# A memory-attention and top-4-of-32 expert step on one core: shorter path from the attention to the first expert, first refills of the weight ring in halves, a reordered last turn

## What is computed (reference, cut)

```python
x = x + mixer(rmsnorm(x, g_mix), ...)
x = x + cross_attn(rmsnorm(x, g_xattn), mk, mv, w_q, w_xo)   # 4 heads of 256
h = rmsnorm(x, g_moe)
logits = h @ w_router + b_router
top_logit, top_e = lax.top_k(logits, 4)
gates = softmax(top_logit)
# for each expert e and its tokens:
gu = xb @ w1[e] + b1[e]; gate, up = split(gu); gate = min(gate, 7); up = clip(up, -7, 7)
y = ((up + 1) * gate * sigmoid(1.702 * gate)) @ w2[e] + b2[e]
x = x + sum(gate weight * y over a token's experts)
return rmsnorm(x, g_final), ...
```

## Time and profile before

| | |
|---|---|
| median of 3 runs | 1202.78 us (1202.31 to 1203.34) |
| the profiled execution, its own time | 1203.28 us |
| its span in the profile | 1201.3 us |
| PE busy | 1162.1 us (97%) |
| weight loads of PE (beside matmuls) | 608.4 us (51%) |
| DVE / ACT / POOL busy | 306.8 / 155.2 / 28.0 us |
| bytes moved by DMA | 458.34 MB, mean 382 GB/s |
| PE's granted clock, mean over the span | 0.998 of full |

### The profile page before, as it was taken

How to read it: one execution, slowest core, us unless ns; L and a number is a source line. 1 busy time by engine, 2 the same in 40 slices (tenths; PEclk the granted TensorE clock), 3 DMA queues, 4 the chain that set the end, 5 groups by cost and what they waited for, 6 DMA issues and landing times.

```text
span 1201.3 us, 14815 instructions
## 1 busy us (share of the span) xinstructions
PE 1162.1 (97%) x5935; PEld 608.4 (51%) x5935; DVE 306.8 (26%) x636; ACT 155.2 (13%) x240; POOL 28.0 (2%) x62
## 2 busy tenths in 40 slices
PE   9999999999999999999999999999999999999986
PEld 8888887684434344444444343434343434343433
DVE  5114532342221212122122212121212121212124
ACT  2011011031101111011011111101110111101012
POOL 0000000000000000000000000000000000000000
PEclk9999999999999999999999999999999999999999
DMA  9963343998999999999999999999999999999994
GB/s 368 400 228 141 117 157 139 427 392 296 423 421 429 427 428 429 428 428 428 428 428 428 429 428 428 429 428 428 429 428 428 428 428 428 429 428 428 427 427 188
DMA packets 39102, 458.34 MB, mean 382 GB/s; under 512 B 5888, under 2 KB 6656, under 8 KB 8096
## 3 DMA queue, kind: packets, MB, share of 16 engines
q1 hardware_dynamic: 36144, 454.12, 90.2%
q10 hardware_dynamic: 2928, 3.80, 0.9%
HBM read 454.41 MB, written 3.23 MB: 381 GB/s over the span
## 4 chain that ended last, share of the span: by engine, by line
PE 51%; DMA 26%; DVE 1%; issue 0%; ACT 0%; SPq 0%; DVEq 0%; ACTq 0%
PE ps L1262 27%; DMA ring<-in_w_gu 26%; PE ps L1357 11%; PE ps L1228 6%; PE ps L1253 4%; PE ps L1272 2%; PE ps L1369 0%; PE ps L1306 0%; DVE resid L1001 0%; DVE arena L987 0%; PE ps L1375 0%; ACT arena L618 0%; DVE arena L929 0%; PE ps L1015 0%; DVE arena L899 0%
## 5 line engine op out<-in xcount | busy, mean ns | idle before, releaser
L1262 PE MATMUL ps<-ring,arena 128*64 128x512 f32 x1536 | 350.4, 598 | 15.5 <-DMA ring<-in_w_gu 11.7
L1262 PEld LDWEIGHTS ps<-ring,arena 128*64 128x64 f32 x1536 | 104.0, 136 | 211.0 <-issue 193.8
L1051 PE MATMUL ps<-arena,ring 128*128 128x264 f32 (+1 forms) x800 | 179.2, 386 | 1.4 <-issue 1.0
L1357 PE MATMUL ps<-ring,arena 128*64 128x512 f32 x768 | 171.1, 594 | 4.0 <-DMA ring<-in_w_dn 3.0
L1051 PEld LDWEIGHTS ps<-arena,ring 128*128 128x128 f32 x800 | 151.6, 190 | 27.2 <-issue 1.6
L1262 PE MATMUL ps<-arena 128*64 128x512 f32 x512 | 116.7, 598 | 4.6 <-DMA arena<-in_w_gu 4.4
L987 DVE COPY arena<-ps 64x512 f32<-64x512 f32 x32 | 22.2, 694 | 365.4 <-PE ps L1357 365.4
L1357 PEld LDWEIGHTS ps<-ring,arena 128*64 128x64 f32 x768 | 54.1, 137 | 112.4 <-issue 99.6
L1228 PEld LDWEIGHTS ps<-arena 128*128 128x128 f32 x768 | 93.2, 197 | 13.8 <-issue 13.8
L938 DVE TENSOR_TENSOR resid<-resid,ps 128x264 f32<-128x264 f32 x128 | 53.2, 429 | 181.4 <-PE ps L1253 180.9
L1228 PE MATMUL ps<-arena 128*128 128x128 f32 x768 | 97.6, 284 | 0.0
(11 more groups left out here) (190 smaller groups left out, 490.9 us busy)
## 6 DMA issues: line engine op xcount, KB each, us to landing
ring<-in_w_gu SPq DMA_DIRECT2D x96, 2048.0 KB, 32.2
ring<-in_w_dn SPq DMA_DIRECT2D x47, 2048.0 KB, 32.7
arena<-in_w_gu SPq DMA_DIRECT2D x32, 2048.0 KB, 32.4
arena<-in_w_dn SPq DMA_DIRECT2D x15, 2048.0 KB, 32.7
ring<-in_w_in SPq DMA_DIRECT2D x10, 1024.0 KB, 27.4
ring<-in_kc SPq DMA_DIRECT2D x8, 1024.0 KB, 4.8
ring<-in_vc SPq DMA_DIRECT2D x8, 1024.0 KB, 5.1
ring<-in_w_v SPq DMA_DIRECT2D x4, 1024.0 KB, 22.6
```

The costliest lines, as they stand in the source:

```text
L1051: last = mm(b[:, 0:width], w[:, k, P * (m % 2):P * (m % 2) + P], source(k), start=(k == 0), stop=(k == KT - 1))
L1262: last = mm(ps[64 * h:64 * h + 64, n, :], tile[:, k, SLOTS * half:SLOTS * half + SLOTS], w[:, at:at + 512], start=(k == 0), stop=(k == KT ...
L1357: last = mm(ps[64 * h:64 * h + 64, 4, :], hid[i % 2][:, k, :], w[:, at:at + 512], start=(k == 0), stop=(k == KT - 1))
```

## The change

**Attention.** Scores go by pairs of heads instead of by token tiles, and the second pair alone waits for the last queries. The first "out" projection waits for the gated convolution piece by piece instead of as a whole. Normalising all four score tiles comes ahead of the samples' maximum. "oS" moves ahead of "o" 6 and 7, which then stand after "oS" and after "oST"; the first "xo" waits for its inputs piece by piece.

**Router.** `g_moe` is multiplied into the router weights early (on DVE, once the parameters are in), so "lg" reads the residual itself, and its last part is cut in four. ACT instead of DVE copies "lg". A square is added as soon as it is there. The table load for the square root is moved ahead of "xo", and the early load for the exponential is dropped. The four chosen logits are now marked by a copy, three `match_replace` and one comparison. The count of tokens per expert becomes a group of matmuls of its own ("free0"). Four PE fillers (`keep_busy`) are dropped. ACT writes `h_tok` in the layout in which the gather reads it.

**First expert.** It writes banks 6 and 7 instead of 0 and 1. The transposition of the gates and the two gathers of the upper half move in between the halves of its second and third units. DVE copies the first gathered quarter ahead of the gates.

**Ring.** The first units are loaded in the order 0, 2, 3, 4, 5, 1, 6, 7. The first eight refills, numbers 8 to 15, all go in two halves of 1 MB, the first half as soon as the first half of the unit before was used.

**Loop.** In even experts the gather stands between the two down units instead of ahead of them.

**Last turn.** Combinations stand one place earlier, so none is left between the last gate/up unit and its transposition. The last down goes to bank 5 and arrives in five pieces (two, two, two, one and one tiles of 128 rows); its result is copied in halves of 256 columns.

```diff
-          + [("o", m) for m in range(4)] + ["pST"] + [("o", m) for m in range(4, 8)] + ["oS", "oST"] + [("xo", m) for m in range(8)]
-          + ["lg", "ssq2", "lgT"] + [("htok", n) for n in range(6)] + ["rank", ...
+          + [("o", m) for m in range(4)] + ["pST", ("o", 4), ("o", 5), "oS", ("o", 6), "oST", ("o", 7)]
+          + [("xo", m) for m in range(8)]
+          + ["lg", ("htok", 0), "ssq2", "lgT"] + [("htok", n) for n in range(1, 6)] + ["rank", ...
...
+LAST_PARTS = [(0, 2), (2, 4), (4, 6), (6, 7), (7, 8)]
...
+            for n in (0, 2, 3, 4, 5, 1, 6, 7):
+                first_units(n)
...
             for n in range(RING_UNITS):
-                first_units(n)
-            sp.wait_ge(half_used, 1)
...
+                for part in range(2):
+                    if part == 0:
+                        sp.wait_ge(half_used, n + 1)
+                    elif n % 4 == 3:
+                        sp.wait_ge(gu_done, n // 4 + 1)
+                    else:
+                        sp.wait_ge(w_used, n - n // 4 + 1)
+                    half = slice(SLOT * part, SLOT * part + SLOT)
+                    sp.dma_start(unit_buffer(n)[:, half], rows_of(RING_UNITS + n)[:, half]).then_inc(
+                        unit_landed[n] if part else half_landed[n], 16)
...
-            TTN(eq[:], lg[:], fourth, ALU.is_equal).then_inc(dve_step, 1)
-            link(nc.vector.tensor_reduce(cnt3, gt[:], AX.X, ALU.add))
+            link(copy(top4[:, :, 0:TOPK], top8[:, :, 0:TOPK]))
             for t in range(TT):
-                ins = nc.vector.tensor_tensor_scan(cum[:, t, :], ones[:, 0:NE], eq[:, t, :], cnt3[:, t:t + 1],
-                                                   ALU.mult, ALU.add)
+                nc.vector.match_replace(struck[:, t, :], top4[:, t, :], logits[:, t, :], -NO_LOGIT).then_inc(dve_step, 1)
...
-            link(STT(eq[:], cum[:], float(TOPK), eq[:], ALU.is_le, ALU.mult))
-            TTN(gt[:], gt[:], eq[:], ALU.add).then_inc(sel_ready, 1)
+            TTN(gt[:], struck[:, :, 0:NE], lg, ALU.not_equal).then_inc(sel_ready, 1)
...
             for u in range(4):
-                if u >= 2:
-                    gather(begin(("ga", u)), 1, range(2 * u - 4, 2 * u - 2)).then_inc(ga_filled, 1)
...
+                halves = gate_up_unit(unit_buffer(u), u, xg[0], 0, FIRST_BANK)
+                next(halves).then_inc(half_used, 1)
+                if u == 1:
+                    turn_gates()
+                if u in (1, 2):
+                    gather(begin(("ga", u + 1)), 1, range(2 * u - 2, 2 * u)).then_inc(ga_filled, 1)
+                next(halves).then_inc(w_used if u < 3 else gu_done, 1)
...
-                    if final and i == 2:
-                        for r in (0, 2):
-                            combine_two(e + 1, i + 1, r)
+                    if early:
                         turn_gate_up(e + 1)
...
+                        if u == 0 and i % 2 == 0 and not (final and i == 2):
+                            gather_half()
```

More of the change, by code:

```diff
@@ L523, in _ @@
         def _(act):
-            for credit in (y_left, side_copied):
+            for credit in (gu_copied, y_left, side_copied):
                 act.sem_inc(credit, 1)
@@ L595, in _ @@
             act.wait_ge(grp, G["oS"] + 1)
+            nc.scalar.activation(warm[:], eps[:], ACT.Sqrt)
             for m in range(KT):
@@ L832, in _ @@
                 TS(top, top, -1.0 / 16.0, None, ALU.mult).then_inc(max_ready, 1)
-            for n in range(2):
+            for n in range(4):
                 normalise(n)
@@ L1126, in _ @@
                     sum_squares("ssq1", 3, T)
-            pe.wait_ge(emptied, G[("q", 7)] + 1)
-            for t in range(2):
-                for pair in range(2):
+            for pair in range(2):
+                pe.wait_ge(emptied, G[("q", 4 * pair + 3)] + 1)
+                for t in range(2):
                     b = begin(("s", t, pair))
@@ L1155, in _, with attend @@
                 last.then_inc(grp, 1)
[L1156 to L1162 removed]
+            def attend(m):
                 b = begin(("o", m))
@@ L1168, in _ @@
                 last.then_inc(grp, 1)
+            for m in range(4):
+                attend(m)
+            b = begin("pST")
+            pe.wait_ge(emptied, G["sS"] + 1)
+            for mt in range(2):
+                last = turn(b[:, P * mt:P * mt + P], s_s[:, P * mt:P * mt + P], ident[:])
+            last.then_inc(grp, 1)
+            attend(4)
+            attend(5)
             b = begin("oS")
@@ L1240, in _ @@
             turns = pe.value_load(iters[0:1, 1:2], min_val=7, max_val=39)
-            b = begin("gT")
-            pe.wait_ge(gate_ready, 1)
-            for t in range(TT):
-                last = turn(b[0:NE, P * t:P * t + P], gate[:, t, :], ident[:])
-            last.then_inc(grp, 4)
             def combine(n, r, m, pair):
```

338 lines of the change are left out of this document (192 added, 146 removed).

## The result

The changed kernel takes **1194.89 us** (median of four runs, 1193.92 to 1195.92), the kernel before in the same comparison 1202.55. The ratio is 0.9932, 95% interval 0.9921 to 0.9944: 7.7 us or 0.7% faster, where 1193.6 was forecast. The profiled execution took 1195.74 us, its span is 1193.9, so 7.4 less than the span before. Medians and ranges in this document leave out two executions in a slow state, one of the kernel with fillers (2021.52 us) and one of the kernel before (3094.72 us).

A forecast was written before the change was run, and what follows sets the result against it. The DMA stream of weights at 428 GB/s was taken as the bound: its start, the bytes left, then the tail. Gains of 3.1 + 1.7 + 2.4 + 2.0 = 9.2 us off 1202.78 gave 1193.6 us, range 1190.5 to 1198.0.

The forecast's parts named there:

- faster: Whole kernel: faster by over 0.2%, that is below 1200.4 us; chance 0.95.
- Term 1: Attention front: fewer PE waits, so PE reaches the last "xo" 3.1 us earlier, bounds 2.0 to 3.7.
- Term 2: From "xo" to the first expert: shorter selection of experts brings the first gate/up matmul 1.7 us earlier, bounds 0.8 and 2.7.
- The clock: Rival: without fillers ahead of rank and gather, PE's clock falls to 1.2 GHz; 16 us lost, 1209.6 us; chance 0.02.
- ahead of 300 us below 1.00: Sign against the prediction: PE's granted clock falls below 1.00 before 300 us.
- Term 3: Ring's first refills in halves: 2.5 us of the stream lost instead of 4.9, a gain of 2.4 us.
- Term 4: Last turn: combinations moved, bank 5 for the last down, result copied in halves; 2.0 us gained, bounds 1.0 and 2.6.
- Half the head: Rival: DVE is late in the front, term 1 and term 2 together give 2.4 us, 1196.0 us; chance 0.12.
- the main case: Whole kernel: the forecast itself, 1193.6 us, holding 1191.5 to 1195.8; chance 0.64.
- Halves run slowly: Rival: the first refills' 16 halves move at 347 GB/s, gain only 2.5 us, 1200.3 us; chance 0.11.
- the rate behind the hole: Sign: in the 50 us after DMA's idle stretch, 407 GB/s or more instead of 386.
- DMA's idle stretch: Sign: DMA's pause between filling the ring and the first refills shrinks from 6 us to about 2.5.

## Why the prediction was right, and where it was not

The forecast was 1193.6 with a range to 1198.0; 1194.89 lies in it, and "faster", at 0.95, is what happened. Its account of the bound held: an earlier start of the stream was found again at the end (4.6 and 4.5; within 0.7 us in the other builds with halves, but for the one with three pieces). But the sum of 9.2 us was 7.7 by the medians and 7.4 by the spans, and its terms did not all hold.

**Term 1** (3.1, bounds 2.0 to 3.7) was 3.8 by the router's start, 3.0 to 4.1 over the builds. Of the 3.7 us of waits in the earlier trace rows 0.7 are left, ahead of the prompt's outputs ("o", waiting for DVE's line 870), where 0.6 were expected to come back. So the waits give 3.0, as forecast, and the rest is the spread of the builds.

**Term 2** (-1.7) is the step that failed. From the router to the first gate/up matmul are 13.3 us instead of 11.85, so 1.5 longer and not 1.7 shorter, a miss of 3.2: about 1.7 of it is the lateness of ACT's copies and 1.6 the clock. The term looked at DVE's steps and PE's register loads, and there it was right: `match_replace` took 0.6 us for all three (0.5 was taken), and in the kernel with ordered writes the way takes 10.1 us, 267.62 - 257.51, with 10.15 forecast. What it left out was the sentence of the change that ACT writes `h_tok` in another layout. It left ACT's copies as they were, at 0.67 us, put nobody's wait down to them, and did not ask what a write of 512 B strides costs. It bounded `match_replace`, which its trace lacked, by two other rows; it did not bound this one. The idle stretch that came of it then let the clock fall.

**The clock** was a rival at 0.02, with the fillers' removal as its cause and 16 us as its price. It did fall, but in the gather alone and at a price of 1.6 us (4.54 against 2.92), since it was back at 1.00 by 270 us, when the first gate/up unit starts. Its cause is shown to be the idle stretch behind ACT's copies: work in it (fillers), or half of it (old selection), keeps the clock. The fillers' removal alone is not the cause. The condition "ahead of 300 us below 1.00", which the prediction named as proof against itself, was met. The Trainium skill (TensorE: Matmul & The Clock Gate, "HAM oscillation — how this bites in real kernels") warns of gaps in the feed from which the next matmuls start cold; the rows here agree that an idle stretch comes first. The waits of its example are longer than the 1.76 us here.

**Term 3** (2.4) has the right size by the account, 7.4 - 5.1 = 2.3, and half its mechanism. The prediction put 2.8 us of the old loss down to refills that find an almost empty queue. With whole refills the stretch of the earlier trace rows moves 433 GB/s instead of 347, so their size is not what made it slow, but when they are issued: 5.8 us apart before. The halves give 1.0, which the spans do not show at the end, and the other 1.2 go, by the argument above, with the waits that the new places and banks take away. The prediction's times at which halves come free already hold that new order (18.2 us for the eighth, and the trace has its issue 17.6 behind the first matmul), yet it booked the whole gain to the halving. Why DMA counts as 0.99 busy at 347 GB/s, whether the queue ran dry or a lone transfer is slow, no run shows.

**Term 4** (2.0, bounds 1.0 and 2.6) was 1.3 by profiles, 1.0 to 2.5 by medians. Behind the last unit it was better than forecast, 2.7 us. But the combinations ahead of it cost 1.4 where 0.3 was taken: eight records are 2.3 us of PE, which in that turn had waits of only 0.8 us for weights to give (0.63 and 0.19 with the old turn). Against the kernel before this does not show, because there PE waited 1.4 + 0.8 + 0.2 us for weights in the same place, and so the trace of the whole change gives 2.9. That the finer pieces give nothing held.

So the forecast was near by compensation: term 2 was 3.2 us too good, term 1 0.7 and the end of the kernel 0.9 too poor, and the medians lie 0.3 us further apart than the spans. "Half the head" (1196.0, chance 0.12) describes what happened better than the main case: its place and size were right, its causes (DVE late, a slow `match_replace`) were not. That the size came out was luck. "Halves run slowly" is out: 419 to 426 GB/s in every stretch of 5 us from 285 to 305 us, and 380 from 275 to 285, where whole refills in a kernel with the same start had 301 and 367.

Of the signs that the prediction named, the rate behind the hole (416 GB/s from 275 to 325 us), the closed gap between the last downs and the shorter wait ahead of the last combinations came. The first gate/up matmul (270.18 for 267.7) and the last unit (4.6 us earlier for 7) came late, and DMA's idle stretch did not shrink to 2.5 us: it now lasts from about 266 to 273.

## What to carry to other kernels

When a change moves a stride from one engine to another, price the operation on the engine that receives it, with the stride on the write and on the read apart, and ask what then waits: here one letter's order in a rearrangement was worth 3 us, more than the 0.9 us of the selection that it hid. Before taking fillers out, look whether something late on another engine will leave TensorE idle at that place. And in a kernel bound by a refilled ring, ask of every small operation not what it costs TensorE but by how much it delays the next free buffer, and look at the end whether the gain arrived: that of the halves did not.

## What was not expected of the hardware

- ACT's copy of 512 float32 per partition from PSUM took 1137 ns (median of six) with neighbouring elements written 512 B apart and 673 to 682 ns with ordered writes, whether PSUM was read in order or with a stride of two elements. The Trainium skill (SBUF — State Buffer, "Door 1: The DMA port swizzle (why `[64,N]` ≈ `[32,N]`)") says that accesses to SBUF which leave a 16-byte line pay, and that PSUM's lines have 8 bytes, with the penalty told for matmuls; the first agrees with the write here, and of the second ACT's read shows nothing.
- The clock fell from 2.4 to 1.2 GHz behind idle stretches of 1.76 and 1.95 us and did not behind 0.89 us. In the kernel before it stayed behind a wait of 1.43 us in the last turn. The same stretch of the same kernel kept it, by the mean clock, in two of nine executions. The length of the wait does not decide alone: with ordered writes PE waits 1.84 us for weights near the start, and the clock is 1.00 in every step of 1 us from 5 to 15 us.

```profile
10.97 3.72 PE L1097 MATMUL ps<-arena,ring 128*128 128x256 f32 x16 [1.84 <-DMA ring<-in_w_k]
```

- From 290 to 305 us, in stretches of 5 us, whole refills of 2 MB ran at 423 to 433 GB/s in two builds of the changed kernel, at 344 to 411 in the kernel before, where they are issued further apart, and halves of 1 MB at 418 to 429 (eleven builds). A lone one was not measured.
